# Memory attention's decode tile: four sequences side by side on 32-column groups in place of two on 64

## What is computed

```
MEM_TOKENS, MEM_HEADS, MEM_HD = 256, 4, 256

def memory_attend(hn, mem_k, mem_v, lw):
    B, T, _ = hn.shape
    q = rmsnorm((hn @ lw['w_mq']).reshape(B, T, MEM_HEADS, MEM_HD), lw['mem_q_norm_g'])
    s = jnp.einsum('bqhd,bkhd->bhqk', q, mem_k.astype(q.dtype), preferred_element_type=jnp.float32) * (MEM_HD ** -0.5)
    p = jax.nn.softmax(s, axis=-1).astype(hn.dtype)
    o = jnp.einsum('bhqk,bkhd->bqhd', p, mem_v.astype(hn.dtype)).reshape(B, T, D_MODEL)
    return o @ lw['w_mo']
...
# decode: cache_mem_k, cache_mem_v are (DEPTH, DEC_BATCH, 256, 4, 256), DEC_BATCH = 8, DEC_SEQ = 16
```

## Time and profile before

| what | value |
|---|---|
| median of 3 runs | 1882.49 us (1879.45 to 1885.01) |
| the profiled execution | 1883.85 us, of which the span of instructions is 1882.5 us |
| PE busy | 1806.0 us (96%) |
| DVE, ACT, POOL busy | 62%, 42%, 39% |
| mean granted TensorE clock | 0.986 |
| memory attention, from its first PE instruction to its last copy | 872.7 to 998.2 us |
| of it the decode tile's scores on PE | 896.3 to 927.3 us |
| of it the decode tile's values on PE | 943.3 to 958.9 us |

### The profile page before, as it was taken

The page is one execution under the profiler, slowest core; times in us unless marked ns, Lnnn a source line. Parts: engine busy times, 40 slices in busy tenths (PEclk is TensorE's granted clock), DMA queues, the critical chain, the costliest instruction groups (busy, mean ns, idle before and its releaser), DMA issues. The chain is left out here.

```text
span 1882.5 us, 27883 instructions
## 1 busy us (share of the span) xinstructions
PE 1806.0 (96%) x10404; PEld 1650.3 (88%) x10404; DVE 1173.3 (62%) x1377; ACT 783.5 (42%) x1491; POOL 742.3 (39%) x638
## 2 busy tenths in 40 slices
PE   6999999989989999999999988999999999999999
PEld 5999999989967788998777878999999999988787
DVE  6235655846665633422525258888788888699985
ACT  5016672325665432412124255444444444444432
POOL 4001220015544350121125117666666666447643
PEclk9999999999979999999999998999999999999999
DMA  6122112151244230113422212222222222496454
GB/s 170 48 58 61 37 45 60 61 160 47 59 142 157 100 135 23 45 68 135 180 79 89 68 35 87 81 70 70 70 70 72 80 70 70 161 347 216 154 173 146
DMA packets 159289, 188.06 MB, mean 100 GB/s; under 512 B 14065, under 2 KB 112986, under 8 KB 158776
## 3 DMA queue, kind: packets, MB, share of 16 engines
q1 hardware_dynamic: 158280, 186.55, 30.5%
q0 software_dynamic: 896, 0.19, 0.1%
q10 hardware_dynamic: 16, 0.00, 0.0%
HBM read 151.64 MB, written 35.07 MB: 99 GB/s over the span
## 5 line engine op out<-in xcount | busy, mean ns | idle before, releaser
L3690 PE MATMUL ffn_banks<-h_parts,up_hi 128*128 128x384 f32 x1920 | 491.5, 337 | 10.4 <-POOL h_parts L4094 4.3
L3690 PEld LDWEIGHTS ffn_banks<-h_parts,up_hi 128*128 128x128 f32 x1920 | 348.2, 189 | 11.8 <-issue 7.3
L3690 PE MATMUL ffn_banks<-h_parts,up_lo 128*128 128x384 f32 x960 | 322.2, 336 | 0.0
L4090 POOL TENSOR_TENSOR up_lo<-up_raw,up_hi 128x512 fp32r<-128x512 f32 x174 | 254.8, 1480 | 136.0 <-ACT up_hi L3852 135.9
L978 PE MATMUL proj_banks<-x_hi,in_w_hi 128*128 128x384 f32 x624 | 214.9, 344 | 0.5 <-DVE x_lo L251 0.5
L978 PE MATMUL proj_banks<-x_hi,in_w_lo 128*128 128x384 f32 x624 | 208.8, 335 | 0.0
L978 PE MATMUL proj_banks<-x_lo,in_w_hi 128*128 128x384 f32 x624 | 208.6, 334 | 0.0
L3690 PEld LDWEIGHTS ffn_banks<-h_parts,up_lo 128*128 128x128 f32 x960 | 181.6, 189 | 0.0
L4141 POOL TENSOR_TENSOR h_parts<-down_cells,h_parts 128x512 fp32r<-128x512 f32 x69 | 108.7, 1583 | 92.6 <-ACT h_parts L3925 92.6
L3811 PE MATMUL ffn_banks<-h_parts,up_hi 128*128 128x512 f32 x352 | 138.3, 393 | 3.7 <-DVE h L4358 2.3
L3814 PE MATMUL ffn_banks<-h_parts,up_lo 128*128 128x512 f32 x352 | 137.1, 390 | 0.0
(11 more groups left out here) (541 smaller groups left out, 3865.4 us busy)
## 6 DMA issues: line engine op xcount, KB each, us to landing
up_raw<-in_w_up SPq DMA_DIRECT2D x44, 512.0 KB, 3.9
down_cells<-in_w_down SPq DMA_DIRECT2D x58, 256.0 KB, 5.6
up_raw<-ffn_gated_rows SPq DMA_DIRECT2D x44, 320.0 KB, 5.9
ffn_gated_rows<-h SPq DMA_DIRECT2D x22, 576.0 KB, 2.8
in_w_raw<-in_w_in SPq DMA_DIRECT2D x24, 512.0 KB, 3.9
up_raw<-ffn_gated_rows SPq DMA_DIRECT2D x44, 256.0 KB, 3.2
spill<-mixT SPq DMA_DIRECT2D x10, 576.0 KB, 3.9
h_kept<-h SPq DMA_DIRECT2D x9, 512.0 KB, 2.8
```

The lines of the kernel that those rows point to most:

```text
L3690: ins = nc.tensor.matmul(banks[:, bank, 0:TC], wt[:, j, k, :], parts[:, q, x, k, :], start=(fresh and n == 1), stop=(n == last), skip_grou ...
L4090: nc.gpsimd.tensor_tensor(w_lo[:, j], weights.full(j), w_hi[:, j].bitcast(F32), ALU.subtract).then_inc(weights.split[j], 1)
```

## The change

The 8 sequences are taken in two sets of four (g = 0, 1; sequences g, g + 2, g + 4, g + 6). The four matmuls of a set write 32 partitions each and use four column groups of 32. A head step now has 16 transposes, 4 copies and 8 score matmuls, and there are 8 head steps in place of 16; the numbers of transposes, copies and matmuls in all are the same. `o_bank` still holds two sequences' turned keys at a time, so PE turns two, scores the head step before, and turns the other two. The turned keys of odd head steps go to tiles 4 and 5 of `attnT`, which are not yet in use.

Sixteen DMAs load all eight key caches at once: six caches into the slots of before, the last two into tiles 1, 2, 3 and `last` of `attnT`, where each row is cut into 8 runs of 512 bytes. The values follow in two sets of four, when all keys of the set have been turned; their wait for `v_used` is gone. `masked` is filled once for each set and never cleared. PE waits for its own last value matmul before it signals `v_used`, which now only releases the load of `mo_w_raw`.

The core of the diff:

```diff
-        STEPS = 2
-        PAIRS, HEAD_STEPS, EARLY = NB // 2, HEADS * (NB // 2), 2
+        STEPS = 2
+        SETS, X = 2, 4
+        HEAD_STEPS, EARLY = HEADS * SETS, 1
...
+        keys_at = [k_one_t[:], attnT[:, :, 4 * P:6 * P]]
+        free_tiles = [attnT[:, :, P * t:P * t + P] for t in (1, 2, 3, last)]
...
-            return slice(64 * x, 64 * x + 64)
+            return slice(32 * x, 32 * x + 32)
...
+            for slot in range(NB):
+                load("cache_mem_k", slot)
+            for slot in range(NB):
+                if slot % X == 0:
+                    sp.wait_ge(k_turned, X * HEADS * (slot // X + 1))
+                load("cache_mem_v", slot)
+            sp.wait_ge(v_used, 1)
             next_weights.load_first(sp)
...
+                    if m >= 2:
+                        pe.wait_ge(k_copied, m - 1)
+                    if n == EARLY and x == 0:
                         pe.wait_ge(out_copied, SAMPLE_AT - 2)
...
-                pe.wait_ge(k_copied, 2 * n + 2)
+                pe.wait_ge(k_copied, X * n + X)
...
-                for n in range(1, HEAD_STEPS):
-                    if n >= EARLY:
-                        turn_keys(n)
-                    pair_scores(out, n - 1)
-                pair_scores(out, HEAD_STEPS - 1)
+                for n in range(EARLY, HEAD_STEPS):
+                    turn_keys(n, (0, 1))
+                    set_scores(out, n - 1)
+                    turn_keys(n, (2, 3))
+                set_scores(out, HEAD_STEPS - 1)
...
-                        if g < PAIRS - 1:
-                            ins.then_inc(v_used, 1)
+                                                           stop=(g == SETS - 1 and kt == 1), skip_group_check=True)
                     ins.then_inc(valued, 1)
+                    pe.wait_ge(valued, i + 1)
+                    pe.sem_inc(v_used, 1)
                     return
...
-                nc.gpsimd.tensor_copy(columns(slot, g), columns(frm, g)).then_inc(masked_ready, 1)
+            def mask(g, frm):
+                def columns(ap):
+                    return ap.rearrange("p f (x c) -> p f x c", x=X)[:, :, :, TB * g:TB * g + TB]
+                nc.gpsimd.tensor_copy(columns(masked[:, g]), columns(frm)).then_inc(masked_ready, 1)
```

More of the change, by code:

```diff
@@ L3007, in memory_attention @@
         block = ph.block()
-        K_SLOT, V_SLOT = (0, 1, 2, 0), (1, 2, 0, 1)
-        K_USE, V_USE = (1, 1, 1, 2), (2, 2, 3, 3)
         third = next_weights.raw
[L3013 to L3020, removed]
+        keys_at = [k_one_t[:], attnT[:, :, 4 * P:6 * P]]
@@ L3022, in cols, with wait_landed @@
+        def wait_landed(engine, slot, use):
+            engine.wait_ge(landed[slot], 32 * use)
         def cols(x):
-            return slice(64 * x, 64 * x + 64)
+            return slice(32 * x, 32 * x + 32)
         @block.sync
         def _(sp):
[L3027 to L3043, removed]
+            def load(name, slot):
+                g, x = divmod(slot, X)
+                for kt in range(2):
+                    frm = A[name][0, SETS * x + g, P * kt:P * kt + P].rearrange("p h d -> p (h d)")
+                    if slot >= 6:
+                        frm = frm.rearrange("p (f c) -> p f c", c=P)
+                    sp.dma_start(cache(slot, kt), frm).then_inc(landed[slot], 16)
@@ L3059, in turn_keys, with set_scores @@
                         for kt in range(2):
-                            ins = nc.tensor.transpose(o_bank[:, 4 * x + 2 * j + kt, :],
-                                                      cache(K_SLOT[g], x, kt)[:, P * (2 * h + j):P * (2 * h + j) + P], C.ident[:])
+                            ins = nc.tensor.transpose(o_bank[:, 4 * (x % 2) + 2 * j + kt, :],
+                                                      part_of(slot, kt, P * (2 * h + j), P), C.ident[:])
                     ins.then_inc(k_turned, 1)
-            def pair_scores(out, n):
+            def set_scores(out, n):
                 g, h = divmod(n, HEADS)
                 pe.wait_ge(masked_ready, g + 1)
-                pe.wait_ge(k_copied, 2 * n + 2)
+                pe.wait_ge(k_copied, X * n + X)
                 for j in range(2):
-                    for x in range(2):
-                        ins = nc.tensor.matmul(out[cols(x), h, :], masked[:, g % 2, 2 * h + j, cols(x)], k_one_t[:, n % 2, x, j, :],
-                                               start=(g == 0 and h % 2 == 0 and j == 0), stop=(g == PAIRS - 1 and j == 1),
+                    for x in range(X):
+                        ins = nc.tensor.matmul(out[cols(x), h, :], masked[:, g, 2 * h + j, cols(x)], keys_at[n % 2][:, 2 * x + j, :],
+                                               start=(g == 0 and h % 2 == 0 and j == 0), stop=(g == SETS - 1 and j == 1),
                                                skip_group_check=True)
@@ L3151, in _ @@
             for n in range(EARLY):
-                turn_keys(n)
+                turn_keys(n, range(X))
             for i in range(NT):
```

80 lines of the change are left out of this document (37 added, 43 removed).

## The result

| | median | runs |
|---|---|---|
| kernel before | 1883.75 us | 4 (1879.45 to 1885.22) |
| kernel after | 1871.64 us | 4 (1869.27 to 1871.97) |

The ratio is 0.9937, with a 95% interval of 0.9923 to 0.9951: faster by 12.1 us, within 9.2 and 14.5 us. The forecast was 11.4 us (1871.1 us), taken from the median of three runs of before, 1882.49 us; with a fourth run that median is 1883.75 us.

What follows compares the result with a forecast made beforehand. PE was taken as the bound in the score and value stages. Values -8.6, scores -2.9 and start +0.1 sum to -11.4 us, from 1882.49 to 1871.1 us; own range 1868 to 1874, wider 1867 to 1878.

Steps and rivals of the forecast that it cites:

- The unit: Scores and values: four records share one slot of 0.216 us, so slots fall from 64 to 32 in each stage.
- The rival of the stretched slot: Scores and values: four groups run but a slot takes 0.252 us, 2.3 us more, 1873.4 us; chance 0.12.
- Two or one group at a time: Scores and values: only two groups at once, 1884.9 us, chance 0.04; or groups of 32 serial, 1912.6 us, chance 0.02.
- Values: Value stage: first to last record falls from 15.37 to 6.75 us, fewer slots and no load wait, gain 8.6 us.
- The loads of the values: Value loads: second set released at about 922, landing by 934 to 945, wanted at about 944; cost taken as 0.
- the two prices of 934 and 945: Last four value loads, 512-byte runs: landed by 934 at 1.26 us each, or by 945 at 3.9 us each.
- Equal latency speaks for nearly equal rate: Value loads: 512-byte runs alone take 3.9 us like 4 KB rows, so cost 0 from a range of 0 to 1 us.
- Scores: Score stretch: head steps of 3.64 us including new waits for DVE's copies, end at 924.4 against 927.33, gain 2.9 us.
- Start of the stage: Early transposes before turn(0): the fourth sequence's cache must have landed (886.8); cost 0 to 0.5 us, taken as 0.1.
- PE's own wait: After the values: PE waits for its last value matmul, hidden by idle before turn_rows; without this cover 0.2 us.
- The clock: Whole stage: the granted clock stays 1.00 throughout, with nothing for it in the sum.
- The rival placed the fall in the score loop: Score loop: waits of 0.7 us in every 3.64 us drop the clock to 1.2 GHz, 1891 us; chance 0.03.

Runs made afterwards that it cites:

- values on 64 columns: Kernel after with each value matmul taking 64 mask columns and writing 64 partitions, so two groups run side by side: 1879.44 us, ratio 0.9982.

## Why the prediction was right, step by step

- **The unit** held: four records in 0.216 us, for scores and values. What shows that the gain is this is the way back: 64 columns gave 6.9 us back in the values and 7.0 us in the scores. The rival of the stretched slot is out; at 0.252 us the values would have taken 7.9 us from first to last record, and they took 6.74. That is 0.054 us a record. The Trainium skill gives about 62 ns per MATMUL as the sequencer's bound (TensorE: Matmul & The Clock Gate, section "Wait — 56ns, not 53.3ns?"), but only with hardware decode off, a condition that the prediction left out and that no row here shows; the bound does not hold in these runs. Its factor of 2.38 for three column groups (same page, "Part 3: Packing small matmuls — row/col tiling") is for three groups at 512 moving columns; four groups at 256 columns in runs of 128 records did 4.0 times the work of one group, with no stretch of the slot. Two or one group at a time is out as well, as long as the groups alternate.
- **Values:** -8.6 forecast, -8.60 measured, of which 6.9 are slots and 1.7 the wait (values on 64 columns). The masks cost nothing: POOL's two copies take 0.61 us each (0.80 us had been forecast) and end at 937.1, before the first value matmul at 937.84:

```profile
935.92 1.17 POOL L3265 COPY mem_masked<-ma_pt 128x512 f32<-128x512 f32 x2
```

- **The loads of the values** were released 26.8 us after turn(1), as worked out, and the last was issued 8.1 us after the first of its set (919.47). SP's timeline, and of the view of the DMAs from 927.8 to 936 us the rate in 40 slices and the time to landing:

```profile
927.53 1.89 SPq L3042 DMA_DIRECT2D mem_attn_t<-in_cache_mem_v  x1
```

```profile
GB/s 295 302 292 285 355 272 275 292 275 295 285 297 300 292 297 292 282 300 292 285 290 290 290 292 287 285 115 48 37 37 37 20 20 17 5 0 0 0 0 0
...
mem_attn_t<-in_cache_mem_v SPq DMA_DIRECT2D x1, 512.0 KB, 7.8
```

  It landed at 935.3, and the second set began at 941.3, so 6.0 us were to spare. The release had come at 919.5 and not at 922, so the two prices of 934 and 945 are better read from the release: 12 and 23 us forecast, 15.8 us measured, nearer the lower one. "Equal latency speaks for nearly equal rate" was not quite right: in this stretch the 512-byte runs moved at about 290 GB/s, a load in 1.8 us, against 410 GB/s in the keys' stretch.
- **Scores:** -2.9 forecast, -2.80 measured. The step of 3.64 us was 3.63 us, with both waits for DVE (the forecast's own terms, 2.91 and 0.71 us, add up to 3.62 us); the first wait, the bare wait ahead of the last score block and the end came within 0.15 us.
- **Start of the stage**, the mis-sized term: +0.1 forecast. The prediction let the fourth sequence's load land 14.0 us after the first score, as before's rows had it (886.8 and 872.79). In the nine profiles with this early block its transposes, which wait for that load, began 14.1 to 14.9 us after it; why it landed later is open. To turn(0) it is 15.02 us on average against 14.69 (+0.33, within its bounds of 0 to 0.5). But in one profile of three (4 of the 9 that have this early block) the clock fell behind these waits and cost 1.6 us more, which the bounds did not hold.
- **PE's own wait** was hidden: `turn_rows` follows turn(4) with no wait.
- **The clock**, the step that failed: "the granted clock 1.00 throughout", a term put at nothing in the sum. The rival placed the fall in the score loop, for 20 us. There the clock stayed 1.00 in spite of 4.35 us idle in 29.19 us. It fell at two other places, behind fewer and longer waits: over score(2), and at the projection, for 1.1 us. Against before, the change's own sum is thus -8.6 - 2.8 + 0.3 + 1.1 = -10.0 us in most executions, 1.6 us less where the clock falls over score(2), and 2.7 us more where before waits longer for its last load. The timed difference of 12.1 us (9.2 to 14.5) does not contradict that, nor does it confirm the 11.4 us more closely than to 2.6 us. That 1871.1 us came within 0.6 us of 1871.64 us is in part luck: the terms left out (0.2 us at the start, 1.1 us and more from the clock) would have made the forecast 1872.4 us or later, and the median of before that it started from was 1.3 us below that of four runs.

## What to carry to other kernels

Put small matmuls on separate column groups, and let their order in the queue alternate between the groups: here two or four of them then took the slot of one. A loop with the group outermost loses most of it (21.6 us for the values here against 6.7 us). When PE gets faster in such a loop, look next at the room that its results go to: here the room for turned keys held back 6 us, half as much as the whole gain, and a bank at rest gave them back. To merge several short waits of PE into a long one was no gain here: in the one profile of it, most of the work behind it ran at half the clock.

## What the runs showed of the hardware

- Four column groups of 32 run at full pace together: 128 records in 6.74 us, 4 within 0.02 us. With the groups one after another, only four records at each border overlapped.
- The clock over score(2) goes with the longest single wait of PE shortly ahead of it. In the 14 profiles it fell where this was 1.89 us or more (1.89, 1.90, 1.90, 1.90 and 3.90), and not where it was 1.70 us or less (the other nine, 1.33 to 1.70). The sum of PE's two waits there orders the profiles in the same way (3.28 to 3.90 us where the clock fell, 2.64 to 3.03 us where it did not), and no run separates the two. For the wait of 2.75 us ahead of the projection this order fails: the clock fell behind it in 9 of 14.
- SP took 8.15 us to issue four loads of 512-byte runs, and 1.92 us for four loads of whole rows, each time right behind four other loads:

```profile
906.71 1.92 SPq L3042 DMA_DIRECT2D mem_v_one<-in_cache_mem_v  x4
...
921.26 8.15 SPq L3042 DMA_DIRECT2D mem_attn_t<-in_cache_mem_v  x4
```

  No engine waited for SP here. What a load right behind them would lose is not shown.
